# One copy of the token rows for gathers and residual in a fused decoder-and-experts kernel, and a sixth weight block kept outside the ring

## The reference, cut to what matters

```python
x = x + g1 * o
h = rms_norm(x, norm2_g) * (1.0 + sc2) + sh2
x = x + g2 * moe_ffn(h, router_w, router_b, w_up, b_up, w_down, b_down)   # top 4 of 32 experts
y = rms_norm(x, final_norm_g)
```

## Time and profile before

| | us |
|---|---|
| median of 3 runs (1135.32 to 1137.63) | 1136.53 |
| the profiled execution, its own time | 1135.78 |
| its span | 1133.9 |
| TensorE busy | 1093.8 |
| VectorE busy | 416.4 |
| ScalarE busy | 186.8 |
| GpSimd busy | 25.2 |

### The profile page before, as it was taken

How to read it: one execution, slowest core, us unless ns; L and a number is a source line. 1 busy time by engine, 2 the same in 40 slices (tenths; PEclk the granted TensorE clock), 3 DMA queues, 4 the chain that set the end, 5 groups by cost and what they waited for, 6 DMA issues and landing times.

```text
span 1133.9 us, 14932 instructions
## 1 busy us (share of the span) xinstructions
PE 1093.8 (96%) x6128; PEld 495.7 (44%) x6128; DVE 416.4 (37%) x873; ACT 186.8 (16%) x383; POOL 25.2 (2%) x57
## 2 busy tenths in 40 slices
PE   7999999999999999999999998999999999999997
PEld 5777678643334333333333333333333333333334
DVE  3167564443333333333323334333333332323334
ACT  1163123211111111111001111111111111111112
POOL 1101100000000000000000000000000000000002
PEclk9999999999999999999999997999999999999998
DMA  9988988899999999999999999999999999999995
GB/s 374 417 335 340 329 295 324 350 391 416 427 416 427 429 427 436 428 431 431 432 431 431 435 429 432 424 425 436 428 432 431 431 430 435 430 431 426 427 427 219
DMA packets 33818, 460.43 MB, mean 406 GB/s; under 512 B 5120, under 2 KB 6144, under 8 KB 12128
## 3 DMA queue, kind: packets, MB, share of 16 engines
q1 hardware_dynamic: 28096, 448.33, 93.8%
q0 software_dynamic: 2688, 9.47, 2.3%
q10 hardware_dynamic: 2976, 1.81, 0.5%
HBM read 454.94 MB, written 4.65 MB: 405 GB/s over the span
## 4 chain that ended last, share of the span: by engine, by line
PE 77%; DMA 21%; DVE 1%; ACT 1%; issue 0%; DVEq 0%; SPq 0%; ACTq 0%
PE bank L1504 30%; DMA ring<-in_w_up 19%; PE bank L1565 15%; PE bank L1118 8%; PE bank L1547 4%; PE bank L1477 4%; PE bank L1372 3%; PE bank L1524 3%; DMA ring<-in_w_ada 1%; PE bank L1079 1%; PE bank L1486 1%; PE bank L1535 1%; PE bank L1722 1%; PE bank L1048 1%; PE bank L1252 0%; PE bank L1335 0%
## 5 line engine op out<-in xcount | busy, mean ns | idle before, releaser
L1504 PE MATMUL bank<-ring,arena 128*64 128x512 f32 x2016 | 453.3, 602 | 16.1 <-DMA ring<-in_w_up 16.0
L1504 PEld LDWEIGHTS bank<-ring,arena 128*64 128x64 f32 x2016 | 142.0, 138 | 316.2 <-issue 287.3
L1565 PE MATMUL bank<-ring,arena 128*64 128x512 f32 x960 | 215.4, 602 | 0.1
L1565 PEld LDWEIGHTS bank<-ring,arena 128*64 128x64 f32 x960 | 67.9, 138 | 126.5 <-issue 126.4
L1118 PE MATMUL bank<-arena,ring 128*128 128x264 f32 x448 | 105.9, 391 | 0.7 <-DVE arena L1831 0.7
L2214 DVE COPY arena<-bank 128x512 f32<-128x512 f32 x32 | 22.1, 692 | 197.3 <-PE bank L1504 197.3
L928 ACT ACTIVATE arena<-bank 128x512 f32<-128x512 f32 x32 | 19.1, 597 | 444.6 <-PE bank L1504 444.6
L2268 DVE TENSOR_TENSOR arena<-bank,arena 128x512 f32<-128x512 f32 x31 | 21.4, 692 | 190.3 <-PE bank L1565 190.3
L1118 PEld LDWEIGHTS bank<-arena,ring 128*128 128x128 f32 x448 | 83.0, 190 | 18.3 <-issue 4.9
L2263 DVE TENSOR_TENSOR arena<-arena,bank 128x512 f32<-128x512 f32 x120 | 74.2, 679 | 0.0
L2223 DVE TENSOR_TENSOR arena<-bank,bupT 128x512 f32<-128x512 f32 x64 | 44.0, 687 | 70.2 <-PE bank L1524 70.2
(11 more groups left out here) (348 smaller groups left out, 688.9 us busy)
## 6 DMA issues: line engine op xcount, KB each, us to landing
ring<-in_w_up SPq DMA_DIRECT2D x41, 4096.0 KB, 29.4
ring<-in_w_up SPq DMA_DIRECT2D x43, 2048.0 KB, 16.5
ring<-in_w_down SPq DMA_DIRECT2D x21, 4096.0 KB, 26.9
ring<-in_w_down SPq DMA_DIRECT2D x17, 2048.0 KB, 14.3
ring<-in_w_ada SPq DMA_DIRECT2D x24, 1024.0 KB, 11.5
ring<-in_w_in SPq DMA_DIRECT2D x12, 1024.0 KB, 11.2
ring<-in_w_o SPq DMA_DIRECT2D x4, 1024.0 KB, 14.0
ring<-in_w_last SPq DMA_DIRECT2D x4, 1024.0 KB, 34.2
```

The source lines that it names most:

```text
L1504: last = mm(bank[64 * half:64 * half + 64, b, :], xe[:, par, k % 4, k // 4, :], src[:, 512 * half:512 * half + 512], start=(k == 0), stop= ...
L1565: last = mm(bank[64 * half:64 * half + 64, b, :], acts[:, k, :], src[:, 512 * half:512 * half + 512], start=(k == 0), stop=(k == KT - 1))
```

## The change

- **Rows.** `h2T`'s prompt part is gone. The rows of `xT` are turned and copied unscaled into `x1tok`. The gathers read them, and `add_up(0)` reads them as the residual; the second turn, its copy to `acc` and the wait for it are gone. The row factor goes into the pick: `pick_of` makes, per half of the tokens, "slot equals rank, times `rst`". `gates_of` makes the gated one-hot from the ranks rather than from the pick. The norm's scale goes, with its shift, into the turned block: `modulated` is eight operations of 56 columns with two per-partition factors, where one operation with an addition stood. `scale2` is spread like the shift is (four more small matmuls, before the output projection).
- **A sixth block outside the ring.** Load 7 (KEPT, a down block of expert 0) goes into memory that `h2T`, `us`, `acc` and others left, two parts early, two after the rows are turned. Its buffer isn't filled again. FIRST_REFILL is now load 11, the aside loads are 8, 9, 19, 20 and 30.
- **Orders.** The fourth sum bank is 2 rather than 6, and waits for `glu_ready`; in `glu` the first clamp stands ahead of `take_tokens`. `ada_copy` comes right after the last task that it depends on. At the end ScalarE takes the sums of squares straight into its logarithms, where VectorE copied and added them before.

```diff
-SUM_BANKS = (4, 7, 5, 6)
+SUM_BANKS = (4, 7, 5, 2)
 ...
-FIRST_REFILL = ASIDE_AT + 2
-ASIDES = (ASIDE_AT, ASIDE_AT + 1, FIRST_REFILL + PAIRS, FIRST_REFILL + PAIRS + 1)
+KEPT = ASIDE_AT - 1
+FIRST_REFILL = ASIDE_AT + 3
+ASIDES = (ASIDE_AT, ASIDE_AT + 1, FIRST_REFILL + PAIRS, FIRST_REFILL + PAIRS + 1, FIRST_REFILL + PAIRS + 11)
+OUTSIDE = (KEPT,) + ASIDES
 ...
 def ring_place(i):
-    return i - sum(i > a for a in ASIDES)
+    return i - sum(i > a for a in OUTSIDE)
 ...
                         load_aside(ASIDES[0])
-                    if i == ASIDES[0]:
+                        sp.wait_ge(sem("Ssam_ready"), NQ * TS)
+                        load_aside(KEPT, (0, 1), aside[2], "kept_in")
+                    if i == KEPT or i in ASIDES[:2]:
+                        continue
+                    if i == FIRST_REFILL:
                         sp.wait_ge(sem("logit_psum"), 1)
                         load_aside(ASIDES[1], (3,))
-                    if i in ASIDES[:2]:
-                        continue
+                        sp.wait_ge(sem("h2tok_psum"), 4)
+                        sp.wait_ge(sem("sq_ready"), KT + 1)
+                        sp.wait_ge(sem("x1s_kept"), 1)
+                        load_aside(KEPT, (2, 3), aside[2], "kept_in")
 ...
-                if task == ("turn", 1):
-                    ada_copy(1)
-                if task == ("turn", 2):
-                    ada_copy(2)
+                if task in (("ada", 1, KT - 1), ("ada", 2, KT - 1)):
+                    ada_copy(task[1])
 ...
-                od.did(A(h2T[:, k, 0:TP], xT[:, k, 0:TP], ACT.Copy, scale=scale2[:, k, 0:1]), sem("u_ready"))
 ...
-            spread_d(8, 1, lambda g: modT[:, 24 + g:32:2, 0:1]).then_inc(sem("crow_psum"), 1)
+            pe.wait_ge(sem("mod_sb"), 7)
+            spread_d(8, 1, lambda g: modT[:, 24 + g:32:2, 0:1])
+            spread_d(16, 1, lambda g: scale2[:, g:KT:2, 0:1]).then_inc(sem("crow_psum"), 1)
 ...
-            for i in range(2):
-                b = 4 + 2 * i
-                for k in range(KT):
-                    last = tr(bank[:, b + k // 4, P * (k % 4):P * (k % 4) + P], xT[:, k, P * i:P * i + P], ident[:, :])
-                last.then_inc(sem("x1tok_psum"), 1)
 ...
+            def pick_of(slots):
+                for i in range(2):
+                    last = TSC(pick[:, i, :], iota_slot[:, :], slots(i), rst[:, i:i + 1], ALU.is_equal, ALU.mult)
+                last.then_inc(sem("pick_ready"), 1)
 ...
+            def modulated(par, blocks, src):
+                dst = xe[:, par].rearrange("p j h s -> p (j h) s")
+                for x in blocks:
+                    last = TSC(dst[:, x, TS:BLK], src[:, x - blocks[0], TS:BLK], sc2p[:, x:x + 1], sh2p[:, x:x + 1], ALU.mult, ALU.add)
+                last.then_inc(sem("xe_ready"), 1)
 ...
                 link(with_bias(tg, 0))
+                v.tensor_scalar(tg, tg, LIMIT, None, ALU.min).then_inc(sem("glu_ready"), 1)
                 if following is not None:
                     take_tokens(*following)
-                v.tensor_scalar(tg, tg, LIMIT, None, ALU.min).then_inc(sem("glu_ready"), 1)
 ...
                     y = acc[i][:, 512 * half:512 * half + 512]
-                    TT(y, y, bank[:, b, :], ALU.add).then_inc(sem("acc_used"), 1)
+                    x = x1tok[:, i, 512 * half:512 * half + 512] if isinstance(n, int) and n == 0 else y
+                    TT(y, x, bank[:, b, :], ALU.add).then_inc(sem("acc_used"), 1)
 ...
-            act.wait_ge(sem("sums_ready"), 3)
-            od.link(A(sumsq[:, 5:8], sumsq[:, 5:8], ACT.Ln, scale=1.0 / D, bias=eps_col[:, 0:1]))
 ...
+            for i in range(2):
+                square_late(i)
+            act.wait_ge(sem("ssq_psum"), 1)
+            od.did(A(sumsq[:, 7:8], bank[:, 2, 0:1], ACT.Ln, scale=1.0 / D, bias=eps_col[:, 0:1]))
+            od.settle()
```

More of the change, by code:

```diff
@@ L225, in load_ahead @@
     r = ring_place(i) - PAIRS
-    return next(j for j in range(r, r + len(ASIDES) + 1) if j not in ASIDES and ring_place(j) == r)
+    return next(j for j in range(r, r + len(OUTSIDE) + 1) if j not in OUTSIDE and ring_place(j) == r)
 def experts(eng):
@@ L401, in build_step @@
         fgs = more[:, 1, 0:512]
-        yout, junk = [ring[:, i, 0:1024] for i in range(2)], [ring[:, 2 + i, 0:1024] for i in range(2)]
-        yfs_out = ring[:, 3, 1024:1536]
+        yout, junk = [ring[:, 4 + i, 0:1024] for i in range(2)], [ring[:, 6 + i, 0:1024] for i in range(2)]
+        yfs_out = ring[:, 7, 1024:1536]
         bd = r_x[:, 512:1024]
@@ L529, in reuse, with load_aside @@
                     sp.wait_ge(sem("states_stored"), 96)
-            def load_aside(i, blocks=range(4)):
+            def load_aside(i, blocks=range(4), place=None, name="aside_in"):
+                if place is None:
+                    place = aside[ASIDES.index(i) % 2]
                 e, t = (i - UPS) // LOADS, (i - UPS) % LOADS
@@ L1447, in gather_half @@
                         c0 = 512 * half + 256 * part
-                        last = mm(bank[64 * half:64 * half + 64, 6 + part, 0:256], pick[:, i, :], h2tok[:, i, c0:c0 + 256],
+                        last = mm(bank[64 * half:64 * half + 64, 6 + part, 0:256], pick[:, i, :], x1tok[:, i, c0:c0 + 256],
                                   start=(i == 0), stop=(i == 1))
@@ L1462, in sample_columns @@
                 pe.wait_ge(sem("h2s_ready"), 1)
-                spread_d(3 * P, TS, lambda g: h2T[:, g:KT:2, TP:T], 4).then_inc(sem("xs_psum"), 1)
+                spread_d(3 * P, TS, lambda g: h2sT[:, g:KT:2, :], 4).then_inc(sem("xs_psum"), 1)
             def sample_logits():
                 for k in range(KT):
-                    last = mm(bank[0:TS, 3, 0:NE], h2T[:, k, TP:T], wrt[:, k, :], start=(k == 0), stop=(k == KT - 1))
+                    last = mm(bank[0:TS, 3, 0:NE], h2sT[:, k, :], wrt[:, k, :], start=(k == 0), stop=(k == KT - 1))
                 last.then_inc(sem("logit_psum"), 1)
@@ L1476, in gather @@
                     for half in range(2):
-                        last = mm(bank[64 * half:64 * half + 64, 6, :], pick[:, i, :], h2tok[:, i, 512 * half:512 * half + 512],
+                        last = mm(bank[64 * half:64 * half + 64, 6, :], pick[:, i, :], x1tok[:, i, 512 * half:512 * half + 512],
                                   start=(i == 0), stop=(i == 1))
@@ L1573, in loads_into @@
             def loads_into(slot, end):
-                return 16 * sum(expert_slot(m) == slot and m not in ASIDES and not comes_with_last(m) for m in range(end))
+                return 16 * sum(expert_slot(m) == slot and m not in OUTSIDE and not comes_with_last(m) for m in range(end))
             def at_load(i, q=0):
+                if i == KEPT:
+                    return -3, 64
                 if i in ASIDES:
                     n = ASIDES.index(i)
-                    return -1 - n % 2, 128 * (1 + n // 2)
+                    return -1 - n % 2, 64 * min(2 * (n // 2) + 2, len(ASIDES))
                 slot = expert_slot(i)
@@ L1751, in _, with sample_squares @@
             combine_into(gpickT_last, ysb_last, *LAST_COLS[3], False)
+            def sample_squares():
+                for part in range(2):
+                    last = mm(bank[:, 2, 0:1], pair[:, :], sumsq_s[:, part:part + 1], start=(part == 0), stop=(part == 1))
+                last.then_inc(sem("ssq_psum"), 1)
+            pe.wait_ge(sem("pair_ready"), 4)
+            pe.wait_ge(sem("squares_ready"), 3)
+            pe.wait_ge(sem("sums_ready"), 1)
+            sample_squares()
             total = LOADS * NE
@@ L1774, in _ @@
                     pe.nop()
+                sample_squares()
                 pe.nop()
-            pe.wait_ge(sem("pair_ready"), 4)
-            pe.wait_ge(sem("squares_ready"), 3)
-            pe.wait_ge(sem("sums_ready"), 1)
-            for part in range(2):
-                last = mm(bank[:, 2, 0:1], pair[:, :], sumsq_s[:, part:part + 1], start=(part == 0), stop=(part == 1))
-            last.then_inc(sem("ssq_psum"), 1)
         @block.vector
@@ new lines, in gates_of, with slots_at, make_gates @@
+            def gates_of(slots, n):
+                for i in range(2):
+                    last = TSC(gpick[:, i], iota_slot[:, :].unsqueeze(1).to_broadcast([P, 2, BLK]), slots(i),
+                               gateE[:, i, bass.ds(n, 1)], ALU.is_equal, ALU.mult)
+                last.then_inc(sem("gpick_ready"), 1)
+            def slots_at(n):
+                return lambda i: rank[:, i, bass.ds(n, 1)]
+            def make_pick(n):
+                pick_of(slots_at(n))
+            def make_gates(n):
+                gates_of(slots_at(n), n)
```

167 lines of the change are left out of this document (70 added, 97 removed).

## The result

The changed kernel takes **1142.07 us** (median of 6 runs, 1141.56 to 1142.35) where the kernel before took 1135.82 beside it (1135.05 to 1137.63). On another chip it was 1142.25 against 1137.06, 1.0041 (1.0027 to 1.0054). It is slower, by 4.9 us by the ratio and 6.25 by the medians. The profiled execution took 1141.57 us, its span is 1139.6.

The account below looks back on a forecast made before the run. Weight transfers were taken to bound the kernel, with TensorE near. Transfers +3.8, last body's stall +0.65 and end -0.5 gave +4.0 us on the median 1136.53: 1140.5 us, range 1138.0 to 1143.6.

Parts of the forecast that it names:

- front: Before load 18's issue: ScalarE's copies no longer hold TensorE (at most -2.2 us), four more spreads cost +0.34; together -1.85.
- stall in a body: TensorE waits for VectorE's turned block before each up block: 0.65 us a body, none to 1.25 by piece price.
- load 18 issued at: SyncE issues load 18 at 269.3 us: load 10's first use at 270.90 today, with TensorE's shifts of -1.6.
- start of an empty queue: From load 18's issue into an empty weights' queue to its first bytes: 0.9 us.
- transfers at the end: Weights' transfers 4.2 us later at load 18, -0.7 for a dip that goes, +0.3 for an aside load: +3.8 us.
- end: After TensorE's last sums, two small VectorE steps go and one small logarithm is added: -0.5 us, between -0.8 and 0.
- The lead is not kept: Load 18 waits for load 10's first use, free aside loads wait behind it; a DMA hole of over ten us opens.
- The pieces at 0.25 us: VectorE's eight operations on the turned block, 56 columns from PSUM, were taken at 0.25 us each.
- The stalls cost nothing until the last wait: Over 30 bodies, 20 us of TensorE stalls fit into 21.7 us of cover, so only the last body's counts.
- Rival 4: TensorE becomes the bound above some 0.7 us of stall a body: 1152 us at 1.25, 1143 at 0.8; chance 0.08.
- Rival 2: The queue still holds bytes at load 18's release, so the hole at 219 us fills free: 1131.8 us; chance 0.06.
- rival 1: The front's gain is taken back by a hidden wait; load 18 issued 1.85 us later, 1142.4 us; chance 0.15.

Follow-up runs that it names:

- Experiment 1: The changed kernel with loads 18 and 19 aside instead of 19 and 20, so load 20 waits in the ring for load 10: 1136.08 us, 0.9990 of before.
- experiment 3: The changed kernel without the sixth block outside the ring, load numbers as before the change: 1136.71 us, 0.9996 of before.
- Experiment 10: The kernel before with only ScalarE's two adaptive-norm copies moved earlier, as in the change: 1134.69 us, 0.9978 of before.
- experiment 7: The changed kernel with loads 18 and 19 aside and the eight pieces replaced by two whole operations over the block: 1130.78 us, 0.9944 of before.
- experiment 9: The changed kernel with four pieces only adding the shift and four only multiplying by a constant, output not the reference's: one execution, 1140.88 us.
- experiment 11: The changed kernel without the sixth block, with two whole operations instead of eight pieces: 1134.75 us, 0.9981 of before.
- experiment 4: The changed kernel with ScalarE's two adaptive-norm copies put back at the tasks before the turns: 1144.62 us, 1.0070 of before.
- 6: The changed kernel with loads 18 and 19 aside and the fifth aside load 28 instead of 30: 1136.51 us, 0.9994 of before.

## Why the prediction was right, point by point

The forecast was slower, 1140.5 us, in a range of 1138.0 to 1143.6; 1142.07 was measured. The mechanism is the one that it names, and most terms are near. The errors didn't cancel: all but one were towards too short a time, and 1.8 of the 5.8 us is their sum. Against the profiled executions:

| term | forecast | measured | from |
|---|---|---|---|
| front | -1.85 | -1.4 | start of the output projection, 178.57 for 179.95 us |
| first block | +0.4 | +0.5 | first up 219.31 for 220.23 us, less the front |
| residual's turn | -0.8 | -0.6 | up(1) of body 0 at 238.68 for 240.23 us, less both |
| stall in a body | 0.65 | 0.84 | chain and waits above |
| load 18 issued at | 269.3 | 270.05 | SyncE's queue |
| start of an empty queue | 0.9 | 1.6 | below |
| transfers at the end | +3.8 | +5.4 | last wait for weights |
| last body's stall | +0.65 | +0.84 | chain |
| end | -0.5 | -0.6 | below |
| sum | +4.0 | +5.8 | 1141.57 for 1135.78 |

- **The lead is not kept** (the step that carries the rest): shown. Load 18 waits for load 10's first use, nothing is issued from 250.0 to 270.05 us, and the queue is dry from 261 us, 3 to 5 us later than "near 256 to 258". Experiment 1 removes the hole by letting the asides past, experiment 3 by leaving the block out, and both remove the loss.
- **Transfers +3.8 us**: the mis-sized term. Its 4.2 us at the hole were 0.75 short at the issue. The start was short too. It came from the landing of one piece into an empty queue, which gives the first byte and not the full rate. The first byte was right: the first packet starts at 270.99 us, 0.94 behind the issue. But from 270 to 273 us 197 GB/s were moved, 0.59 MB, for which 430 GB/s would have needed 1.4 us. So the rate begins, in effect, at 271.6 us, 1.6 us behind the issue. The dip at 324 us went as said (431 GB/s for 333), and the lag fell from 5.4 us at 90 MB to 4.5 at 110. So behind the dip the transfers are 4.5 to 4.8 us late for the 3.8 of the forecast, up to 440 MB. The last wait for weights ends 5.4 us later because 432.3 MB had been moved by then, and 432.0 before; that makes 0.7 us, and why is open. The 1.5 us from last byte to landing is an estimate in the prediction. For load 17 of before the packet records give 1.6: what the queue has moved by its end (82.9 MB, read where nothing follows it, in the kernel after) is moved at 265.89 us, and it lands at 267.53. For the piece of the earlier trace rows they give 0.6 to landing, after 2.0 of transfer rather than 1.2 and 0.96 from issue to first packet. The 1.5 us stands on both sides of the 4.2 and cancels.
- **The front** was right in cause. Its rival, that the gain is taken back, has a part: of the 2.2 us that the copies free, 1.56 are left behind VectorE's state updates, which entered the chain (TensorE's line 1275 starts at 163.32 us, its line 1268 of before at 164.88), and one wait of 0.7 us for them is new. The four more small spreads cost 0.2 us, not 0.34. Experiment 10 shows the move by itself to be worth 2.0 us.

```profile
PE bank L1323 <- DVE ring L2014: 0.7, 1, 0.7
```

- **The pieces at 0.25 us, a stall of 0.65**: the piece was met (0.244). The stall came out 0.2 longer because TensorE is ready earlier: its gated sum, which took 2.09 us, takes 1.92, as experiment 7's chain shows at the same place; why, no experiment separates. VectorE was as forecast, from the clamp's start (263.92) to the block's end (266.31) 2.4 us. The prediction took the piece from its own rows, nearest to the 0.27 us of the one with 128 columns and one factor. That it came out right doesn't mean that such a row is the measure: in experiment 9 a piece with one per-partition factor takes 0.183 us from start to start, and one with none 0.122.
- **The stalls cost nothing until the last wait**: right for this kernel. 25.1 us of stalls came, and 12.9 us of waits for weights were still left, so the cover was far larger than the 21.7 us that the prediction counted. TensorE was busy 1077.7 us, 16 less than before. Some 7 of it are the gated sums, all 30 together (before, then after):

```profile
L1547 PE MATMUL bank<-arena,gpickT 64*128 64x512 f32 x240 | 67.6, 628 | 0.0
L1557 PE MATMUL bank<-arena,gpickT 64*128 64x512 f32 x240 | 60.6, 619 | 0.0
```

  Another 1.9 us is the residual's second turn, and some 7 are TensorE's clock (last section). Rival 4's threshold of "some 0.7 us a body" was therefore too low: at 0.84 TensorE wasn't the bound.
- **The end, -0.5**: from the last sum on VectorE to its first product of rows, 1131.26 to 1133.84 us in the chain, 2.6 us, were 3.2 before. ScalarE's small steps follow each other without the two of the earlier trace rows:

```profile
1131.26 0.43 DVE arena L2369
...
1132.32 0.29 ACT sumsq L1026
...
1133.40 0.18 ACT sumsq L1031
...
1133.60 0.21 ACT sumsq L1033
...
1133.84 0.75 DVE ring L2432
```

- **Rival 2 (lead kept, 1131.8)** was rightly put low for the change as written. Its arithmetic was nearly right for a kernel with another order of issue: experiment 7 gives 1130.8. In part that is luck: it leaves out the front's 2.0 us and prices the block at 4.9, where experiment 11 gives 4.0. What I didn't see, and experiment 1's expectation of 1132.5 to 1135 missed by 1 us or more, is that such a lead also needs a TensorE without stalls. My reading: with the lead, the buffers are full and each stall delays a release that the queue is waiting for; without it, the same stalls hide behind late transfers. The stalls were worth 2.7 us in the changed kernel and 5.2 with the hole filled. The intervals of these two (0.6 to 4.9, 2.6 to 7.6) overlap, so the times alone don't show it. The transfers do: at 140 MB taking the stalls out wins 1.2 us in the changed kernel and 3.6 with the hole filled.
- **The range's upper end, 1143.5**, is not worked out by the terms given: rival 1 and a stall of 0.15 us more, ahead of load 18 and at the end, come to 1142.7. Nothing rests on it.

What stays open: why the gated sum is shorter, where the last 0.7 us of the transfers' lateness comes from, and how much of experiment 4's 3 us beyond the 2.3 of its profile is scatter (its six runs lie between 1143.42 and 1145.78 us).

## What to carry to other kernels

A new buffer outside a ring is worth what it fills only if the order of issue keeps its lead: number the loads so that none whose place is free stands behind one that waits. Look for the next thin place of the queue before counting a gain. Where transfers and compute are as near to each other as here (before, the weights' queue filled 93.8% of the span and TensorE was busy for 96%), a stall's price can depend on which of them is late: price it again after each repair. Here the same stalls cost more transfer time once the transfers led (3.6 us at 140 MB for 1.2). Per-partition factors on small operations had a price of their own (0.061 us each, over 56 columns); where a block can be treated whole, two passes with broadcast rows were cheaper here (1.3 us) than eight pieces with two factors (2.04 us).

## What the runs showed of the hardware

- Half of a small piece's time on VectorE was its two per-partition factors: 0.122 us without, 0.061 more for each, over 56 fp32 columns out of a bank.
- An empty queue took 0.94 us from issue to first packet (270.05 to 270.99 us), and 1.6 us in effect until it moved at the full rate.
- The granted clock of TensorE fell less often where it stalled a little in every body. The stalled kernels (after, twice, and experiments 1, 3, 4 and 6) have two stretches at a granted clock of 0.5 of full speed, one near 700 us and one at the very end. All seven others have these and 3 to 7 more of 3.4 us. In the kernel before, one begins 0.7 us behind a wait of 2.5 us for weights:

```profile
583.72 8.78 PE L1504 MATMUL bank<-ring,arena 128*64 128x512 f32 x32 [2.54 <-DMA ring<-in_w_up]
```

```profile
584.00:589.00 5.00, 5.00 (x18) 1.51 (x16) 0.00 (x0) 0.00 (x0) 0.00 (x0) 0.66 1.00 433
```

The 32 matmuls take 8.78 us there, and 7.09 in the chains above: 1.7 us for each such stretch. In the changed kernel the longest wait for weights is 1.4 us, and the same window stays at a granted clock of 1.00:

```profile
584.00:589.00 5.00, 3.67 (x20) 1.06 (x16) 1.35 (x2) 0.00 (x0) 0.00 (x0) 1.00 0.98 419
```

Four such stretches of before, gone after, are 7 of the 16 us by which TensorE was less busy, and so part of the cover that I hadn't counted. In the six stalled profiles no wait for weights is longer than 1.4 us; in the seven others the longest is 2.2 to 2.6. Whether the length of the single wait is what matters, or something else that goes with the stalls, no experiment separates. The stretch near 700 us also differs between executions of one kernel: 10.2 us in one profile of the changed kernel, 17.1 in the other.
